# An fp32 encoder layer: first chunk normalised after its projections, earlier query loads, convolution steps dealt by VectorE's work, and the query/key scale spread as two fp32r matmuls

## The reference, cut to what matters

```python
def _layer(x, ...):                      # x: 512 prompt tokens, and 2048 sample tokens; 1024 features
    h = _rms(x, norm1_g)
    proj = h @ w_in                      # 14 column tiles of 128: k, 4 x q, v, 4 x (gate, a)
    q = _rms(q.reshape(B, T, 8, 64), q_norm_g); k = _rms(k.reshape(B, T, 2, 64), k_norm_g)
    attn = _window_attention(q, k, v, attn_sink)      # window +-128, ALiBi, sink
    u = a * jax.nn.sigmoid(gate)
    u = _dwconv(u, conv_dw_w, conv_dw_b)              # 31 taps, 512 channels
    u = jax.nn.silu(_layernorm(u, conv_ln_g, conv_ln_b))
    x = x + jnp.concatenate([attn, u], axis=-1) @ w_out
    h2 = _rms(x, norm2_g)
    g = jax.nn.silu(_dwconv(h2 @ ffn_w_gate, ffn_dw_w, ffn_dw_b))   # 3 taps
    return x + (g * (h2 @ ffn_w_up)) @ ffn_w_down     # 2816 wide
```

## Time and profile before

| | us |
|---|---|
| median of 3 runs (lowest to highest) | 2833.62 (2830.11 to 9411.69) |
| the profiled execution | 2833.89 |
| its span, first to last instruction | 2832.1 |
| PE busy in it | 2747.4 (97%) |
| DVE busy | 1812.5 (64%) |
| ACT busy | 1315.0 (46%) |
| mean granted TensorE clock | 0.992 of full |

### The profile page before, as it was taken

One profiled execution on the slowest core, in us unless ns is written; L12 is line 12 of the kernel. 1 busy time (PEld: TensorE's weight loads), 2 busy tenths in 40 slices (PEclk: granted clock), 3 DMA queues, 4 the chain that ended last, 5 costly groups with the idle time before them and its releaser, 6 DMA issues.

```text
span 2832.1 us, 34669 instructions
## 1 busy us (share of the span) xinstructions
PE 2747.4 (97%) x13326; PEld 2394.0 (85%) x13326; DVE 1812.5 (64%) x2821; ACT 1315.0 (46%) x1958; POOL 183.0 (6%) x312
## 2 busy tenths in 40 slices
PE   5999999999899999999999999999999999999998
PEld 4766666778788989888998879988899999999998
DVE  2476864789668778568777578785364554545453
ACT  4365565456535356546446436446243333333231
POOL 0100101110100000100000110000000000000000
PEclk9999999999999999999999999999999999999999
DMA  7444435553464443553443743444644433343333
GB/s 182 156 146 153 156 124 206 167 177 116 133 220 138 135 150 126 202 175 118 164 136 111 247 150 113 158 133 140 223 142 155 134 121 112 123 160 133 113 112 99
DMA packets 136756, 421.86 MB, mean 149 GB/s; under 512 B 24496, under 2 KB 37296, under 8 KB 134032
## 3 DMA queue, kind: packets, MB, share of 16 engines
q1 hardware_dynamic: 112624, 339.86, 37.0%
q0 software_dynamic: 23968, 79.79, 8.1%
HBM read 353.81 MB, written 65.77 MB: 148 GB/s over the span
## 4 chain that ended last, share of the span: by engine, by line
PE 87%; DVE 5%; ACT 3%; DMA 3%; issue 2%; POOL 0%; SPq 0%; DVEq 0%; ACTq 0%; POOLq 0%
PE bank L1352 40%; PE bank L1368 20%; PE bank L1324 11%; PE bank L1338 7%; PE bank L1424 2%; PE bank L1445 2%; PE bank L1434 2%; DVE wlo L996 1%; DVE cc L1062 1%; PE bank L1411 1%; DMA wraw<-w_out_t 1%; PE bank L1394 1%; DVE xs L1014 1%; ACT whi L727 1%; DMA qt<-q_scratch 1%
## 5 line engine op out<-in xcount | busy, mean ns | idle before, releaser
L996 DVE TENSOR_TENSOR wlo<-wraw,whi 128x1024 fp32r<-128x1024 f32 x506 | 617.0, 1219 | 366.6 <-ACT whi L727 366.2
L1352 PE MATMUL bank<-hw_hi,whi 128*128 128x430 f32 (+1 forms) x2112 | 765.5, 362 | 0.0
L1352 PE MATMUL bank<-hw_hi,wlo 128*128 128x430 f32 (+1 forms) x2112 | 757.0, 358 | 0.0
L1352 PE MATMUL bank<-hw_lo,whi 128*128 128x430 f32 (+1 forms) x2112 | 756.8, 358 | 0.0
L727 ACT ACTIVATE whi<-wraw 128x1024 fp32r<-128x1024 f32 x506 | 533.9, 1055 | 472.0 <-DMA wraw<-w_down_t 266.2
L1368 PE MATMUL bank<-mid,whi 128*128 128x428 f32 x2112 | 587.3, 359 | 0.0
L1352 PEld LDWEIGHTS bank<-hw_hi,whi 128*128 128x128 f32 x2112 | 399.1, 189 | 39.7 <-issue 23.3
L1368 PEld LDWEIGHTS bank<-mid,whi 128*128 128x128 f32 x2112 | 394.4, 188 | 28.7 <-issue 12.7
L1062 DVE SCALAR_TENSOR_TENSOR cc<-win,par,cc 128x512 f32<-128x512 f32 x600 | 415.7, 744 | 0.0
L1352 PEld LDWEIGHTS bank<-hw_lo,whi 128*128 128x128 f32 x2112 | 399.9, 189 | 17.4 <-issue 1.0
L1352 PEld LDWEIGHTS bank<-hw_hi,wlo 128*128 128x128 f32 x2112 | 398.1, 188 | 15.3
(11 more groups left out here) (127 smaller groups left out, 2683.1 us busy)
## 6 DMA issues: line engine op xcount, KB each, us to landing
wraw<-w_ffn_t SPq DMA_DIRECT2D x264, 512.0 KB, 3.5
wraw<-w_down_t SPq DMA_DIRECT2D x132, 512.0 KB, 3.5
wraw<-w_in_t SPq DMA_DIRECT2D x70, 512.0 KB, 3.7
wraw<-w_out_t SPq DMA_DIRECT2D x40, 512.0 KB, 3.7
hw_raw<-h_scratch SPq DMA_DIRECT2D x24, 430.0 KB, 4.6
yb<-x_scratch SPq DMA_DIRECT2D x48, 214.0 KB, 3.6
y_t<-yb POOLq DMA_DIRECT2D x48, 214.0 KB, 3.1
xt<-x_tok SPq DMA_DIRECT2D x20, 512.0 KB, 6.1
```

The costliest lines, as they stand in the source:

```text
L996: nc.vector.tensor_tensor(wlo[n % RING][:], wraw[n % RING][:], whi[n % RING][:].bitcast(F32), ALU.subtract) \
L1352: mm = nc.tensor.matmul(out, l[:, k, :], r[:, k, 1:TC + 1] if s else r[:, k, :], start=(k == 0 and j == 0), stop=(k == KT - 1 and j == 2))
```

## The change

1. The first chunk is multiplied unscaled. x is loaded once, feature-major, into `x0` in four pieces (`load_first`); ACT makes `h_hi` straight from it with norm1_g as its scale (`first_high`) and squares it (`first_squares`); DVE makes `h_lo` (`first_low`) and adds the squares (`first_add`). After tile 0 one fp32 matmul with `ones` (`first_sum`) gives the sums, ACT turns them into `rs0` with Ln and Exp (`first_scale`, at slot 1), and DVE multiplies the outputs of chunk 0 by it while it takes them out of PSUM (`first_eviction`; for the gated unit a second multiplication in `glu`). The four `xt` loads, `spread_scale` and `rs1` of chunk 0 go, and `ones` is a memset. PE has one wait for the constants' loads behind `first_sum`.
2. `load_q` moves from one slot ahead of the block to three, for all blocks but the first two.
3. The convolution steps are dealt in proportion to `conv_room`, what is left of a slot after DVE's other tasks by a table `WORK`; the first chunk's steps start at slot 12 instead of 16.
4. The inverse root is split, `q_hi` by ACT (`qk_high`) and `q_lo` by DVE (`qk_low`), both at b+9; `qk_spread` becomes two fp32r matmuls, and waits for `q_lo`.

```diff
-CONV_AT = {0: (16, 47), 1: (58, 96), 2: (108, 165), 3: (181, 240), 4: (256, 312)}
+CONV_AT = {0: (12, 47), 1: (58, 96), 2: (108, 165), 3: (181, 240), 4: (256, 312)}
...
     DVE_SIDE[_b + 8].append(("qk_inverse", _c))
+    ACT_SIDE[_b + 9].append(("qk_high", _c))
+    DVE_SIDE[_b + 9].append(("qk_low", _c))
...
-    POOL_SIDE[_b - 1].append(("load_q", _c, _n))
+    POOL_SIDE[_b - 1 if _N < 2 else _b - 3].append(("load_q", _c, _n))
...
+def conv_room(n):
+    kind = SLOT[n][0]
+    tile = {"A": 0.4, "O": 1.8, "G": 2.1, "D": 0.6}[kind]
+    if n + AHEAD < SLOTS:
+        tile += 1.6
+    return max((7.3 if kind in "AO" else 6.2) - tile - sum(WORK.get(t[0], 0) for t in DVE_SIDE[n]), 0.4)
...
-            CONV_OPS_AT[_x + _i] = (_at + PAIR_OPS * _i // _m, _at + PAIR_OPS * (_i + 1) // _m)
+        for _i in range(_y - _x + 1):
+            CONV_OPS_AT[_x + _i] = (_at + _done[_i], _at + _done[_i + 1])
...
+            def first_squares(p):
+                act.wait_ge(s_x0[p], 16)
+                if p > 1:
+                    act.wait_ge(s_x0a, p - 1)
+                dst = x0_sq if p > 0 else x0_acc
+                nc.scalar.activation(dst[:], x0[:, PK * p:PK * (p + 1), :], ACT.Square).then_inc(s_x0q, 1)
+
+            def first_high(p):
+                act.wait_ge(s_x0[p], 16)
+                for k in range(PK * p, PK * (p + 1)):
+                    hi = nc.scalar.activation(h_hi[0][:, k, :], x0[:, k, :], ACT.Copy, scale=col("g1", k))
+                hi.then_inc(s_hhi, 1)
...
+            def first_eviction(f):
+                dve.wait_ge(s_used, f + 1)
+                dve.wait_ge(s_rs1, 1)
+                src = bank[out_bank(OUTPUT["A", 0, f])]
+                if f < NORMED:
+                    nc.vector.tensor_tensor(qk[f][:], src[:], rs0[:], ALU.mult).then_inc(s_qc, 1)
...
-                pe.wait_ge(s_qri, c + 1)
+                pe.wait_ge(s_qil, c + 1)
...
-                nc.tensor.matmul(bank[A_MISC][:], spread[0:NORM_ROWS, P * m:P * (m + 1)], q_inv[0:NORM_ROWS, :],
-                                 start=True, stop=True).then_inc(s_qsp, 1)
+                for i, r in enumerate((q_hi, q_lo)):
+                    mm = nc.tensor.matmul(bank[A_MISC][:], spread[0:NORM_ROWS, P * m:P * (m + 1)], r[0:NORM_ROWS, :],
+                                          start=(i == 0), stop=(i == 1))
+                mm.then_inc(s_qsp, 1)
...
-            pe.wait_ge(s_par, 32)
-            spread_scale(0)
-            pe.wait_ge(s_par, 16 * 7)
+            pe.wait_ge(s_set, 4)
             for n in range(SLOTS):
...
                     project(n, c, f)
+                    if n == 0:
+                        first_sum()
+                        pe.wait_ge(s_const, 16 * 5)
```

More of the change, by code:

```diff
@@ L227 @@
     _mid = (_f + _l) // 2
+    _sum = [sum(conv_room(n) for n in range(_f, m)) for m in range(_f, _l + 1)]
+    _mid = next(_f + i for i, v in enumerate(_sum) if v >= _sum[-1] / 2)
     for _pair, (_x, _y) in enumerate(((_f, _mid - 1), (_mid + 2, _l))):
         _at = PAIR_OPS * (2 * _c + _pair)
-        _m = _y - _x + 1
+        _room = [conv_room(n) for n in range(_x, _y + 1)]
+        _done = [round(PAIR_OPS * sum(_room[:i]) / sum(_room)) for i in range(len(_room) + 1)]
         POOL_SIDE[_x - 2].append(("load_window", _c, _pair))
-        for _i in range(_m):
-            CONV_OPS_AT[_x + _i] = (_at + PAIR_OPS * _i // _m, _at + PAIR_OPS * (_i + 1) // _m)
+        for _i in range(_y - _x + 1):
+            CONV_OPS_AT[_x + _i] = (_at + _done[_i], _at + _done[_i + 1])
 SHARED = {}
@@ L241 @@
 SHARED = {k: v + 1 for k, v in SHARED.items()}
-SHARED["norm1", 0] = 0
 C_PICK = 2 * P
@@ L391, in encoder_layer @@
         s_dn = sem("down_output_ready")
+        s_const = sem("tables_loaded")
+        s_x0 = [sem(f"first_x_loaded{p}") for p in range(PIECES)]
+        s_x0q = sem("first_x_squared")
+        s_x0a = sem("first_x_added")
+        s_x0m = sem("first_x_sum_ready")
+        s_x0l = sem("first_x_log_ready")
+        s_sigin = sem("first_gate_scaled")
+        s_u0 = sem("first_glu_unscaled")
         s_xt = [sem(f"x_tokens_loaded{i}") for i in range(2)]
@@ L768, in qk_square @@
                 src = bank[out_bank(OUTPUT["A", c, m])]
-                nc.scalar.activation(qk[m][:], src[:], ACT.Copy).then_inc(s_qc, 1)
+                if c == 0:
+                    act.wait_ge(s_qc, m + 1)
+                    src = qk[m]
+                else:
+                    nc.scalar.activation(qk[m][:], src[:], ACT.Copy).then_inc(s_qc, 1)
                 nc.scalar.activation(q_sq[M % 2][:], src[:], ACT.Square).then_inc(s_qs, 1)
@@ L777, in qk_root, with qk_high @@
                                      bias=eps[0:NORM_ROWS, 0:1], scale=1.0 / HEAD_DIM).then_inc(s_qrt, 1)
+            def qk_high(c):
+                act.wait_ge(s_qri, c + 1)
+                nc.scalar.activation(q_hi[0:NORM_ROWS, :], q_inv[0:NORM_ROWS, :], ACT.Copy).then_inc(s_qih, 1)
             def v_copy(c):
@@ L795, in sigmoid @@
                     act.wait_ge(s_u, CT * c + j - 1)
-                nc.scalar.activation(sig[j % 2][:], bank[out_bank(OUTPUT["A", c, f])][:], ACT.Sigmoid).then_inc(s_sig, 1)
+                if c == 0:
+                    act.wait_ge(s_sigin, j + 1)
+                src = sig[j % 2] if c == 0 else bank[out_bank(OUTPUT["A", c, f])]
+                nc.scalar.activation(sig[j % 2][:], src[:], ACT.Sigmoid).then_inc(s_sig, 1)
             def exps(N, t):
@@ L920, in mid_high @@
                 nc.scalar.activation(mid[:, i, 0, :], cv[J % 2][:], ACT.Copy).then_inc(s_mhi, 1)
-            act.wait_ge(s_set, 3)
-            for b in range(BLOCKS):
-                token_squares(0, b)
-            token_root(0)
+            act.wait_ge(s_set, 4)
+            act.wait_ge(s_par, 16)
+            first_high(0)
             weight_high(0)
-            scale_copy(0)
-            for p in range(PIECES):
-                h_high(0, p)
-                if p == 1:
-                    weight_high(1)
+            first_squares(0)
+            for p in range(1, PIECES):
+                first_high(p)
+                first_squares(p)
+            weight_high(1)
+            act.wait_ge(s_const, 16 * 5)
+            nc.scalar.activation(spread[:], spread_raw[:], ACT.Copy).then_inc(s_sprd, 1)
             for n in range(SLOTS + 1):
@@ L934, in _ @@
                 now = SLOT[n] if n < SLOTS else (None,)
+                if n == 1:
+                    first_scale()
                 if before[0] == "A":
@@ L1383, in spread_scale, with first_sum @@
                 mm.then_inc(s_nst, 1)
+            def first_sum():
+                pe.wait_ge(s_x0a, PIECES)
+                nc.tensor.matmul(bank[A_MISC][:], ones[:], x0_acc[:, 0, :], start=True, stop=True).then_inc(s_x0m, 1)
             def qk_sum(c, m):
```

174 lines of the change are left out of this document (110 added, 64 removed).

## The result

| | before | after |
|---|---|---|
| median, us | 2832.77 | 2787.65 (2786.16 to 2788.76) |
| the profiled execution, us | 2833.89 | 2786.16 |
| its span, us | 2832.1 | 2784.4 |

The ratio is 0.9843, with a 95% interval of 0.9824 to 0.9863: 1.6% less, within the 2% of the middle class ("same"). One execution of the kernel before took 9411.69 us and is not in the ratio. The two profiled executions differ by 47.7 us, where 58.7 was forecast. So 11 us of the expected gain are to be found.

What follows compares the result with a forecast made beforehand. TensorE, busy 2747.4 us or 97% of the span, was taken as the bound. Gains of 22.8 + 13.7 + 17.5 + 1.2 + 3.5 = 58.7 us off 2833.9 gave 2775.2, with a range from 2755 to 2799.

Steps and rivals of the forecast that it cites:

- The start: Start of the kernel: TensorE starts at 10.6, tile 1 at 20.9 instead of 43.70, worth 22.8 us (bounds 17 and 25).
- The spread's price: Spreads in the chunks: two fp32r matmuls save 0.78 us each, 25 times, 19.5; 13.7 after new waits.
- The bound (1.25): Upper bound for the new spread: 1.25 us, if 10 rows in fp32r cost what the fp32 one does.
- The waits for `q_lo`: Spreads: TensorE waits for the low part about 6.6 us in chunk 1, 1.5 in chunk 0, hardly in 2 and 4.
- Rival B: The wait for `q_lo` binds in every chunk; 22 us comes back, 2797; chance 0.20.
- Chunk 0: Slots 1 to 13: 3.1 us of new waits against 3.9 of spread savings, a gain of 0.8.
- Query loads and dealing: Earlier loads end waits at blocks 9, 13, 17, worth 17.5 us; convolution steps leaving heavy DVE slots, 1.2 and 3.5.
- the 8.1 and 8.8 of chunk 1: Chunk 1's long wait with its clock loss: old 8.1 us, new 8.8; with 3.9 of saving, gain 3.2.
- The sum of chunk 1: Wait for the layer norm's sum, 8.4 us with clock loss: some 3 left, gain 3.5 (bounds 0 and 8.4).
- Rival A: The dealing breaks the DVE and ACT loops, remaining waits go: about 22 us more off, 2753; chance 0.16.
- Rival D: Slower: VectorE's room is overrated, 155 moved convolution steps lie on TensorE's path, 115 us, 2890; chance 0.03.
- The table load: ACT's table switch: no added drain of 1.38 us; with it, chunk 0's chain to `q_lo` and the total 1.4 higher.

Runs made afterwards that it cites:

- undo_spread: The changed kernel with the old spread again: one fp32 matmul from the inverse, no high and low part; 2794.67 us, ratio 0.9870.
- pick128: The changed kernel with the sum of squares of a query or key written over 128 output rows, not 10, by zero columns; 2784.71 us, ratio 0.9827.
- split_dve: The changed kernel with the inverse's high part made by VectorE right behind the inverse, the low part right behind that; 2785.14 us, ratio 0.9825.
- norm_early: As split_dve, with the query or key normalisation also put ahead of the weight's low part in VectorE's order; 2783.37 us, ratio 0.9821.
- gate_wait: The changed kernel with chunk 0's sigmoids waiting only for VectorE's scaled gate, one wait less; 2786.00 us, ratio 0.9828.

## Why the prediction was right and where it wasn't

The time fell as forecast, and 2787.65 lies inside 2755 to 2799, 12 us from 2775. On the class the prediction had hardly taken a side (0.49 for within 2%, 0.48 for over 2% faster, its own point at 2.07%), so that it came out is no credit. By its steps:

- **The start** was right: first matmul 10.6 (10.6), the sum waited for 19.3 (19.6), tile 1 at 20.50 (20.9), 23.2 for 22.8. It was built from ACT's pieces, and those set it.
- **The spread's price** is the step that failed. "Two fp32r matmuls of 512 columns cost 2 x 0.23" took the starts of neighbours of one shape for those of a matmul with 10 rows among matmuls with 128. Measured is 0.86 for a spread, 0.39 saved and not 0.78: 25 x 0.39 = 9.8 in place of 19.5. Of the 10 us missing in the five chunks this makes 7.7 (1.9 each in chunks 0, 2 and 4, 1.5 in chunk 1, 0.5 in chunk 3), and `undo_spread` agrees: 7.0 for 13.7. The other 2.3 are chunk 0's, below. The 0.4 are the two changes of shape; they stood in the 1.25 of before as well (0.84 for the matmul itself in `pick128`, and 0.4), and I subtracted a sum without them. The bound (1.25) held. With 0.39 in chunks 2 and 4, 2.0 comes out, and 2.0 was measured in both.
- **The waits for `q_lo`**: 6.6 in chunk 1 (6.62), 1.5 in chunk 0 (1.17), none in 2 and 4, as said. In chunk 3 2.4 and 5.4 stand for the forecast of one wait of some 7, together 7.8. Rival B is refuted, since chunks 2 and 4 have none.
- **Chunk 0** was forecast at plus 0.8 and came to minus 3.4. Of the 4.2 between them the spread's price makes 1.9. The wait for the root grew by 2.1 and not 0.7, since the change moved DVE's product ahead of the sigmoid and the table load came to wait for it: 1.4. The stretch at the lower clock behind it makes 1.5; it was not forecast, and other kernels with the same wait don't have it. The wait for `q_lo` was 0.4 shorter than forecast, and the 3.1 of new waits was 0.3 more than its own terms (0.7, 1.5 and 0.6).
- **Query loads and dealing**: 18.2 and 4.6 by place for 17.5 and 4.7, but by cause this was wrong, though the sum was right. "Moved ahead of all [...] it lands some 5 us early or more. Then the scores go at once" holds only with the dealing; alone it is worth 1.4. The sentence that asked whether the bias would be late next, and answered by the steps that leave those slots, held the whole mechanism. I booked the gain to the other part, and that 17.5 came so near is luck in part: the two changes were made together. In block 8, put down at nothing, waits of 1.78, 0.66 and 0.56 became one of 3.25 with its loss of clock: -1.9. (By its own terms the forecast was 12.0 + 0.3 + 5.1 = 17.4; and the 8.1 and 8.8 of chunk 1 are more than its waits of 5.58 and 6.6 with the 1.7 of clock make, 7.3 and 8.3. Neither moves the time by over 0.5.)
- **The sum of chunk 1**: 3.56 left for "some 3", 2.2 gained for 3.5. Rival A is out, since the loops stayed. Rival D too: even dealing is the slower one, by 20.
- **The table load**: the next activation starts 1.30 after it here too (60.50 to 61.80). The Trainium skill (ScalarE: Activation LUTs, "What ACT_TABLE_LOAD costs") adds a drain of some 1.38; again this trace doesn't show it, and the wait for `q_lo` in chunk 0 was shorter than forecast, not longer.

## What to carry to other kernels

Price a small matmul from the starts around it, its neighbours' included: if it differs in rows or columns from them, widening it by zeros can make it cheaper, and a second part may ride in the zero rows. Before booking a gain to a moved load, ask who is late with it: here relieving the engine that the load's queue waited for brought 16.6, and moving the load 1.4 to 4.5. A table by place can't tell two such edits apart; the four kernels with and without each can. And a wait that one removes on a loop is worth only its distance to the next wait on that loop: 10.2 us of waits for `q_lo` went, and 2.5 us came of it.

## What the hardware showed that I had not expected

- A matmul of another shape than its neighbour's, in rows (10 for 128) or in columns written (10 for 128), starts 0.2 us late on each side, and its weight load begins with it and not a start ahead. Zeros to 128 took it away: slot 13 from 6.40 to 6.03, slot 4 from 6.74 to 6.41 (0.17 on a side for columns). The matmul itself takes no longer with 128 rows: 0.23 from start to start. The Trainium skill (TensorE: Matmul & The Clock Gate, "The mechanism", under "What overlaps and what doesn't") has a weight load overlap a running matmul only where their groups of rows differ. These rows speak against it: the load runs ahead where the rows are the same, and not from 128 to 10.
- With two waits ahead of an activation that needs a new table, the table load (60.50) began only when the last was over. With one wait it went ahead (53.95); TensorE's wait behind this went from 2.75 to 1.42.
- A stretch at the lower clock (some 1.55 us lost) is not tied to the wait ahead of it. Behind the same wait of 2.75 to 2.79 us slot 8 has a granted clock of 0.76 in the changed kernel and of 1.00 in `undo_spread`, `split_dve` and `norm_early`; behind the same 1.2 us slot 10 has 1.00 in the changed kernel and 0.79 in `gate_wait`. What decides it stays open, so a gain of that size in one trace is not proof of an edit.
